# High and low halves of the MLP input side by side: one 512-column matmul in three of fourteen half units

## The reference, cut to what matters

```
h2 = rmsnorm(x, g_mlp[l])
u = jax.nn.relu(jnp.einsum('bsd,df->bsf', h2, w_ff1[l]))
x = x + jnp.einsum('bsf,fd->bsd', u * u, w_ff2[l])
return rmsnorm(x, g_final)
```

## Time and profile before

| | us |
|---|---|
| median of 3 runs | 364.74 (364.2 to 365.33) |
| span of the profiled execution | 363.0 |
| TensorE busy | 356.1 (98%) |
| VectorE busy | 287.4 (79%) |
| ScalarE busy | 231.8 (64%) |

### The profile page before, as it was taken

How to read it: one execution, slowest core, us unless ns; L and a number is a source line. 1 busy time by engine, 2 the same in 40 slices (tenths; PEclk the granted TensorE clock), 3 DMA queues, 4 the chain that set the end, 5 groups by cost and what they waited for, 6 DMA issues and landing times.

```text
span 363.0 us, 5565 instructions
## 1 busy us (share of the span) xinstructions
PE 356.1 (98%) x2109; PEld 310.9 (86%) x2109; DVE 287.4 (79%) x404; ACT 231.8 (64%) x384; POOL 40.9 (11%) x62
## 2 busy tenths in 40 slices
PE   8999999999999999999999999999999999999993
PEld 7998889887788888888888899999999999999983
DVE  4877973958877777487587879999998888998584
ACT  5996436987565675064466657777677777665424
POOL 1341000000000100000021011111101111220002
PEclk9999999999999999999999999999999999999999
DMA  8999567665341366328165999999999998963003
GB/s 263 382 388 311 221 187 239 214 225 166 134 142 38 106 233 228 116 89 325 51 212 168 273 334 221 279 301 293 287 267 268 278 280 248 294 171 116 2 0 116
DMA packets 42198, 76.77 MB, mean 212 GB/s; under 512 B 1924, under 2 KB 19345, under 8 KB 41921
## 3 DMA queue, kind: packets, MB, share of 16 engines
q1 hardware_dynamic: 37840, 66.59, 53.6%
q0 software_dynamic: 4176, 9.64, 13.4%
q10 hardware_dynamic: 160, 0.27, 0.2%
HBM read 75.44 MB, written 1.05 MB: 211 GB/s over the span
## 4 chain that ended last, share of the span: by engine, by line
PE 96%; DMA 1%; DVE 1%; ACT 0%; issue 0%; POOLq 0%; DVEq 0%; SPq 0%; POOL 0%; ACTq 0%
PE ps L1413 29%; PE ps L1415 29%; PE ps L1414 29%; PE ps L1420 4%; PE ps L1611 2%; PE ps L1636 2%; DMA raw<-in_w_in_dram 1%; ACT prob L560 0%; PE ps L1498 0%; PE ps L1527 0%; PE ps L1522 0%; PE ps L1532 0%; DVE xs L1172 0%; POOLq L129 0%; DVE qkT_b L1403 0%
## 5 line engine op out<-in xcount | busy, mean ns | idle before, releaser
L544 ACT ACTIVATE whi<-raw 128x1024 fp32r<-128x1024 f32 (+3 forms) x127 | 119.6, 989 | 14.7 <-PE ps L1415 13.4
L944 DVE TENSOR_TENSOR wlo<-raw,whi 128x1024 fp32r<-128x1024 f32 (+2 forms) x64 | 69.9, 1127 | 25.4 <-ACT whi L544 25.3
L1413 PE MATMUL ps<-whi,xT_hi 128*128 128x512 f32 (+2 forms) x188 | 73.4, 390 | 0.0
L1415 PE MATMUL ps<-whi,xT_lo 128*128 128x512 f32 (+2 forms) x188 | 71.3, 379 | 0.0
L1414 PE MATMUL ps<-wlo,xT_hi 128*128 128x512 f32 (+2 forms) x188 | 71.2, 378 | 0.0
L1415 PE MATMUL ps<-xT_hi,wlo 128*128 128x256 f32 x224 | 63.4, 283 | 0.0
L1414 PE MATMUL ps<-xT_lo,whi 128*128 128x256 f32 x224 | 63.4, 283 | 0.0
L1413 PE MATMUL ps<-xT_hi,whi 128*128 128x256 f32 x224 | 63.3, 283 | 0.0
L1413 PE MATMUL ps<-whi,lat_hi 128*128 128x512 f32 (+2 forms) x134 | 51.7, 385 | 0.0
L1414 PE MATMUL ps<-wlo,lat_hi 128*128 128x512 f32 (+2 forms) x134 | 51.2, 382 | 0.0
L1415 PE MATMUL ps<-whi,lat_lo 128*128 128x512 f32 (+2 forms) x134 | 51.1, 382 | 0.0
(11 more groups left out here) (157 smaller groups left out, 499.9 us busy)
## 6 DMA issues: line engine op xcount, KB each, us to landing
raw<-in_w_ff_dram SPq DMA_DIRECT2D x32, 1024.0 KB, 7.2
raw<-in_w_in_dram SPq DMA_DIRECT2D x14, 1024.0 KB, 6.3
raw<-in_w_out_dram SPq DMA_DIRECT2D x4, 1024.0 KB, 5.1
t_raw<-in_w_ff_dram SPq DMA_DIRECT2D x12, 256.0 KB, 7.9
raw<-in_w_ff_dram POOLq DMA_DIRECT2D x12, 256.0 KB, 4.8
t_raw<-in_w_ff_dram POOLq DMA_DIRECT2D x12, 256.0 KB, 7.2
gates<-in_b_gate_dram POOLq DMA_DIRECT2D x2, 1024.0 KB, 6.8
raw<-in_w_o_a_dram SPq DMA_DIRECT2D x2, 1024.0 KB, 5.1
```

Source lines behind the costliest of these rows:

```text
L544: return nc.scalar.activation(dst, src, ACT.Copy, scale=scale)
L944: nc.vector.tensor_tensor(wlo[:, s, h * w:(h + 1) * w], raw[:, s, h * w:(h + 1) * w], whi[:, s, h * w:(h + 1) * w].bitcast(F32), ALU.subtr ...
L1413: nc.tensor.matmul(dst, a_hi, b_hi, start=start, stop=False)
L1415: return nc.tensor.matmul(dst, a_lo, b_hi, start=False, stop=stop)
```

## The change

The two tiles `xT_hi` and `xT_lo` become one tile `xT` of [P, KT, 2, SEQ], in which for each k the 256 high and the 256 low columns are neighbours. In the half units of `WIDE`, (1,0), (1,1) and (7,1), `mlp_in_wide` replaces `mlp_in_unit`: a step of k is one matmul of 512 columns, `whi` by [hi | lo], and one of 256 columns, `wlo` by hi, which accumulates onto the left half of the bank. The two blocks f no longer share bank 4 but take a bank each (`WIDE_BANKS`: 7 and 4, 6 and 4, 4 and 5), since each needs all 512 columns. The right half (whi by lo) is copied out to `prob` by ScalarE (`wide_parts`), VectorE adds it to the left half (`wide_sums`), and ScalarE's Relu and Square follow from SBUF (`wide_square`); in (7,1) VectorE does relu and square in one instruction instead. A new wait on TensorE guards bank 6: product P4 of the first `mlp_products` waits for `u_sum` 2, VectorE's first add of (1,1).

```diff
@@ -104,6 +104,11 @@
 FAST = FF_CHUNKS - 1
+WIDE = ((1, 0), (1, 1), (FAST, 1))
+WIDE_BANKS = ((7, U_BANK), (6, U_BANK), (U_BANK, P1))
+FIRST_BLOCKS, SECOND_BLOCKS = slice(0, 4, 3), slice(1, 3)
 def rope_tables(dim):
     half = dim // 2
@@ -139,8 +144,7 @@
         wlo = sb("wlo", [P, SLOTS, SLOT_W], F32R)
         xs = sb("xs", [P, TT, D], F32)
-        xT_hi = sb("xT_hi", [P, KT, SEQ], F32R)
-        xT_lo = sb("xT_lo", [P, KT, SEQ], F32R)
+        xT = sb("xT", [P, KT, 2, SEQ], F32R)
         lat_hi = sb("lat_hi", [P, 8, SEQ], F32R)
         lat_lo = sb("lat_lo", [P, 8, SEQ], F32R)
         qkT_b = sb("qkT_b", [P, 2, 8, SEQ], F32)
@@ -176,6 +180,7 @@
         ps = ctx.enter_context(nc.psum_tensor("ps", [P, 8, HALF], F32))
+        xT_hi, xT_lo = xT[:, :, 0, :], xT[:, :, 1, :]
         N_MIX, N_CQ, N_CKV, N_MLP, N_FIN = 0, 2, 4, 6, 8
         R_QA, R_QB = 10, 12
         SSQ_MLP, SSQ_FIN = 6, 10
@@ -846,6 +855,21 @@
                 act.wait_ge(u_act, c * 2 + p + 1)
                 nc.scalar.activation(rows[:, 2 * p + 1, :], prob[:, p, :], ACT.Square).then_inc(u_sq, 1)
+            def wide_parts(i):
+                c, p = WIDE[i]
+                for f in range(2):
+                    act.wait_ge(*(u_done, c * 2 + p + 1) if f else (u_wide, i + 1))
+                    copy(prob[:, 2 + f, SEQ:HALF], ps[:, WIDE_BANKS[i][f], SEQ:HALF]).then_inc(u_corr, 1)
+            def wide_square(i):
+                c, p = WIDE[i]
+                act.wait_ge(u_act, c * 2 + p + 1)
+                nc.scalar.activation(prob[:, p, :], prob[:, p, :], ACT.Relu).then_inc(u_relu, 1)
+                act.wait_ge(u_relu, i + 1)
+                nc.scalar.activation(rows[:, 2 * p + 1, :], prob[:, p, :], ACT.Square).then_inc(u_sq, 1)
             def lefts_high(c, p):
                 act.wait_ge(w2_used, c * 2 + p - 1)
                 act.wait_ge(s_part, c * 6 + 3 * p - 3)
@@ -865,8 +889,13 @@
                     lefts_high(c, 0)
                 high_blocks(c, 1)
                 high_t24(c, 1)
-                relu_square(c, 1)
-                high_t3(c, 1)
+                if first:
+                    wide_parts(1)
+                    high_t3(c, 1)
+                    wide_square(1)
+                else:
+                    relu_square(c, 1)
+                    high_t3(c, 1)
                 high_w1(c + 1, 1)
                 lefts_high(c, 1)
                 if last:
@@ -893,7 +922,8 @@
             high_t24(1, 0)
             high_t3(1, 0)
             high_blocks(1, 0)
-            relu_square(1, 0)
+            wide_parts(0)
+            wide_square(0)
             mlp_chunk(1, first=True)
             with act.Fori(2, FAST - 1) as c:
                 mlp_chunk(c)
@@ -902,7 +932,7 @@
             act.wait_ge(w2_used, 2 * FAST)
             copy(p1_copy, ps[:, P1, :]).then_inc(p1_read, 1)
             high_last(1)
-            relu_square(FAST, 1)
+            wide_parts(2)
             u_high(1)
             def final_act(t, n):
@@ -1319,6 +1349,21 @@
                                                in1=prob[:, p, :], op0=ALU.max, op1=ALU.mult)\
                     .then_inc(u_sq, 1)
+            def wide_sums(i):
+                p = WIDE[i][1]
+                z = prob[:, p, :].rearrange("p (b s) -> p b s", b=4)
+                for f, blocks_of in enumerate((FIRST_BLOCKS, SECOND_BLOCKS)):
+                    dve.wait_ge(u_corr, 2 * i + f + 1)
+                    nc.vector.tensor_tensor(
+                        z[:, blocks_of, :],
+                        ps[:, WIDE_BANKS[i][f], 0:SEQ].rearrange("p (t s) -> p t s", t=TT),
+                        prob[:, 2 + f, SEQ:HALF].rearrange("p (t s) -> p t s", t=TT), ALU.add).then_inc((u_sum, u_act)[f], 1)
+                if i == 2:
+                    dve.wait_ge(u_act, 2 * FF_CHUNKS)
+                    nc.vector.scalar_tensor_tensor(out=rows[:, 2 * p + 1, :], in0=prob[:, p, :], scalar=0.0,
+                                                   in1=prob[:, p, :], op0=ALU.max, op1=ALU.mult).then_inc(u_sq, 1)
             def mlp_chunk(c, first=False, last=False):
                 left_sums(c, 0)
                 if first:
@@ -1330,7 +1375,12 @@
                     lefts_low(c, 0)
                     low_w1(c + 1, 0, (1,))
                 block_sums(c, 1)
-                low_w2(c, 1)
+                if first:
+                    low_blocks(c, 1, c * 8 + 4 - 8)
+                    wide_sums(1)
+                    low_sums(1, c * 8 + 4 - 6)
+                else:
+                    low_w2(c, 1)
                 left_sums(c, 1)
                 low_w1(c + 1, 1, (0,))
                 lefts_low(c, 1)
@@ -1361,6 +1411,7 @@
             low_sums(0, 0)
             low_blocks(1, 0, 2)
             add_rows0(0)
+            wide_sums(0)
             mlp_chunk(1, first=True)
             with dve.Fori(2, FAST - 1) as c:
                 mlp_chunk(c)
@@ -1368,6 +1419,7 @@
             u_low(0)
             combine_banks()
             low_last(1)
+            wide_sums(2)
             u_low(1)
             combine_rows()
@@ -1729,6 +1781,24 @@
                         m = product(dst, whi[:, s, w], wlo[:, s, w], h_hi, h_lo, k == 0, k == KT - 1)
                 return m
+            def mlp_in_wide(i):
+                c, p = WIDE[i]
+                s = (U_FF + p) % SLOTS
+                pe.wait_ge(w1_lo, c * 4 + 2 * p - 2)
+                for f, bank in enumerate(WIDE_BANKS[i]):
+                    if bank == U_BANK:
+                        pe.wait_ge(u_act, c * 2 + p)
+                    if bank == P1:
+                        pe.wait_ge(p1_read, 1)
+                    for k in range(KT):
+                        w = slice(k * 256 + f * P, k * 256 + (f + 1) * P)
+                        nc.tensor.matmul(ps[:, bank, :], whi[:, s, w], xT[:, k, :, :].rearrange("p a s -> p (a s)"),
+                                         start=(k == 0), stop=False)
+                        m = nc.tensor.matmul(ps[:, bank, 0:SEQ], wlo[:, s, w], xT_hi[:, k, :], start=False,
+                                             stop=(k == KT - 1))
+                    m.then_inc((u_wide, u_done)[f], 1)
             def mlp_out_rows(t, p):
                 s = (U_FF + 2 + p) % SLOTS
@@ -1774,6 +1844,8 @@
                 for bank, a, b in PRODUCTS:
                     if first and bank in ROW_BANK:
                         pe.wait_ge(rows0_read, ROW_BANK.index(bank) + 1)
+                    if first and bank == WIDE_BANKS[1][0]:
+                        pe.wait_ge(u_sum, 2)
                     a = slice(a * P, (a + 1) * P)
                     if b < T3:
                         w = slice(b * HALF, (b + 1) * HALF)
@@ -1822,14 +1894,17 @@
                     if t == 1:
                         m.then_inc(w2_used, 1)
                         if p == 0:
-                            mlp_in_unit(1, 0)
+                            mlp_in_wide(0)
                     elif p == 0:
                         turn_u(1)
                     else:
                         m.then_inc(rows0_done, 1)
             def mlp_chunk(c, first=False, end=False):
-                mlp_in_unit(c, 1)
+                if first:
+                    mlp_in_wide(1)
+                else:
+                    mlp_in_unit(c, 1)
                 mlp_products(c, 0, first)
                 mlp_in_unit(c + 1, 0)
                 mlp_products(c, 1, False, end)
@@ -1838,7 +1913,7 @@
             with pe.Fori(2, FAST - 1) as c:
                 mlp_chunk(c)
             mlp_chunk(FAST - 1, end=True)
-            mlp_in_unit(FAST, 1)
+            mlp_in_wide(2)
             pe.wait_ge(last_lo, 2)
             pe.wait_ge(uT_lo_done, 3)
             mlp_out_last(0, 0, 0)
```

More of the change, by code:

```diff
@@ L266, in hybrid_block @@
         u_sq = sem("u_sq")
+        u_wide = sem("u_wide")
+        u_corr = sem("u_corr")
+        u_sum = sem("u_sum")
+        u_relu = sem("u_relu")
         u_turned = sem("u_turned")
```

## The result

The changed kernel takes 371.84 us (median of 4, 371.18 to 372.17) against 364.61 (median of 4): ratio 1.0196, 95% interval 1.0184 to 1.0209, 7.2 us slower. The forecast was slower, at 369.6 with a range of 368.5 to 371.3; the time lies 0.5 us above the range.

A forecast was written before the change was run, and what follows sets the result against it. TensorE, busy for 98% of the span, was taken to bound the kernel. The net stall of 4.35 us and 0.51 at the end gave 364.74 + 4.86 = 369.6 us, range 368.5 to 371.3 for 8 in 10.

The forecast's parts named there:

- The saving of a half unit: Each wide half unit: 16 steps, each 0.012 us shorter, so 0.19 us saved, 5.56 instead of 5.75 us.
- The Trainium skill's rule that was weighed: Weights load during the previous matmul, 2.5 ns issue gap: 48 matmuls fewer would give 0.12 us; forecast took 0.58.
- The shift of VectorE: From `left_sums(1,0)` on, VectorE's work moves 1.28 us later, from 212.64 to 213.92.
- The step that decides: P4 behind (1,1) waits for VectorE's first add to free bank 6: TensorE still 4.7 us, net 4.35 late.
- all else keeps its cover: Behind the stall, (2,0)'s weights and (1,1)'s sums come at most 2.5 us later, TensorE asks 4.35 later.
- The end: Behind (7,1), the chain through VectorE's residual add and ScalarE's scaling and squares ends 0.51 us later.
- The second small gap: 18 matmuls behind (7,1), TensorE waits for the split of the last u: a stall of 0.33 us.
- The clock: Forecast: full clock throughout. Rival, chance 0.22: it falls in the stall before P4, giving 370.8 to 371.3 us.
- The rival's price: Matmuls at 1.2 GHz behind a clock fall in the stall cost 1.2 to 1.7 us more; chance 0.22.
- The rival of an early add: VectorE reaches (1,1)'s first add before TensorE needs bank 6: 364.9 or 364.2 us, no slowdown; chance 0.06.

The follow-up runs named there:

- grouped: Changed kernel with (1,1)'s copies and adds earlier, (7,1) narrow, and each block's eight 512-column matmuls ahead of its eight 256-column ones; 365.47 us.
- fill_18: Changed kernel plus 18 matmuls of 512 columns, no part of the result, in the gap between P1 and P4's wait; 370.36 us.
- wait_alone: Kernel before, all half units narrow, with only one more wait: first-pass P4 waits for w2_lo 8; 371.55 us.
- changed_again: The changed kernel unaltered, measured and traced a second time; 372.68 us, ratio 1.0207.
- early_add: Changed kernel with (1,1)'s block 0 copied ahead of high_blocks and added ahead of the residual adds, block 1 behind them; 365.47 us.

## Why the prediction was right and wrong, point by point

**The saving of a half unit** (0.19 us each): mis-sized, 0.11. The distances of starts, 0.120 and 0.228, were right for runs of equal widths, and grouped shows the 5.56 that they give. A 256-column start behind a 512-column one comes 0.235 to 0.24 after it. The Trainium skill's rule that was weighed, "TensorE: Matmul & The Clock Gate" (Part 2), which gave 0.12 us for all three half units, is not borne out: the changed trace gives 0.33. (That section gives the 2.5 ns for a matmul by itself.)

**The shift of VectorE** (1.28 us): `left_sums` started 213.74 - 205.29 = 8.45 us behind (1,0)'s start, before 7.25: 1.20, right.

**The step that decides** (TensorE still for 4.7 us, net 4.35): right, within 0.3. The 4.65 of the tables is from start to start and holds the 0.23 of a matmul; still for want of bank 6 TensorE stood for 4.42, and P4 started 19.15 us behind (1,0)'s start, before 14.95: 4.20 late. fill_18, where the clock stays full, has 4.19 there and 4.32 at (2,0), as the first matmul behind the wait is 0.34 and not 0.23 ahead of the next. That all else keeps its cover was right too: the loop behind it takes 115.93 us to (7,1) in the changed trace and 115.94 in before's.

**The end** (+0.51): +0.42 against (7,1)'s start, by the path described: residual add behind VectorE, squares behind ScalarE's scaling. The 0.09 less stand already at VectorE's split of the last u, which began 9.13 us behind (7,1)'s start (355.34), worked out 9.23. The second small gap is there, TensorE's starts being 0.45 instead of 0.23 apart at 356.18; it stands still for 0.22 there, worked out 0.33.

**The clock: here the prediction failed.** The step: the sum of 369.6 has TensorE go on at the full clock behind the stall, with no term for slower matmuls; they were a rival at a chance of 0.22. The runs show 1.6 to 2.8 us there, each time. The chance rested on one row, full clock 5.14 us after the last matmul, "longer than my gap and speaks against it". One such row gives one draw of a delay that differs from execution to execution. In wait_alone the clock fell at about 223.2, 3.0 us after TensorE's last matmul had ended, in changed_again after 3.5, and in the changed kernel's first trace after 4.9, when work had been resumed for 0.6 us. The ends of the twelve traces show the same spread: the clock fell 2.5 to 5.3 us after the last matmul of the program had ended, and the row that I went by, the 5.3 of before, is the longest of all. In the trace of wait_alone, where the last matmul ended at 364.06, the clock (third from the end) is full until 366.4 and at half from 366.6 on:

```profile
364.10:366.40 2.30, 0.00 (x0) 0.00 (x0) 1.19 (x4) 1.80 (x7) 1.35 (x3) 1.00 0.29 109
366.60:369.70 3.10, 0.00 (x0) 0.00 (x0) 0.35 (x1) 0.25 (x1) 0.00 (x0) 0.50 0.70 254
```

All 12 executions with this gap and nothing in it show a mean clock of 0.982 to 0.994, those of before 0.995 to 0.999. The rule of the Trainium skill that was quoted there ("TensorE: Matmul & The Clock Gate", Part 1), that the monitor's windows run freely, agrees with this variation from execution to execution; I had taken it for a minority of runs, or all, and it was all, by the mean clocks; three of the twelve have a trace. That such windows are the cause is not shown by any run.

**The rival's price** (1.2 to 1.7 us) was mis-sized as well. It was taken from the start of the program, which shows how long the first climb took there. Measured: 1.63 and 2.81 us, by the length of the stretch; what decides between the two lengths is not known. Had the rival been the forecast at 369.6 + 1.6 to 2.8, it would have been 371.2 to 372.4, around the measured 371.84. The sum from the traces: 4.32 + 2.8 + 0.42 = 7.5 for the long stretch and 6.4 for the short, with 7.2 measured.

The rival of an early add was wrong for this kernel, but right as a recipe: early_add is that case.

## What to carry to other kernels

A result that frees a resource of the bounding engine belongs ahead of all work in the helper's queue that the engine asks for later; the place of two 0.4 us adds and their copies was worth 6.4 us here. When you move it forward, look at what then comes late: here the cover that was left was 0.25 us. When you cost a stall of TensorE like those here (4.3 us without a matmul: the clock fell in 12 of 12 executions; 3.1 us: in some of 4), add the matmuls at half rate behind it, take no comfort from a single late fall of the clock in a trace, and do not take the length of the slow stretch from the program's start. Before merging matmuls to save weight loads, look at the distance of starts: here it was some 7 to 12 ns a merge, 0.3 us in all, which two helpers' extra work in a tight queue outweighs at once; even with the stall gone no version was faster.

## What the runs showed of the hardware that was not expected

The granted clock fell 3.0 to 4.9 us after the last matmul ahead of the gap had ended, once with TensorE at work again, and 2.5 to 5.3 us after the last one of the program. In the gap's case it stayed at half for 3.4 or 6.8 us; at half, 512-column matmuls start 0.43 us apart instead of 0.228. Within one program both lengths occur. And a mixed row of widths is slower than the widths apart: 0.352 us for a pair of 512 and 256 columns in turn, 0.347 grouped.
